# A two-layer transformer block: more convolution taps on TensorE, over shifted copies of the input, and a gate chunk moved ahead

## The reference, cut to what matters

```python
def odd_mixer(h, w_in, dw_w, dw_b, ln_g, ln_b, w_out):
    proj = h @ w_in                                     # [512, 3 * 1024]
    a, b, gate = jnp.split(proj, [CONV_WIDTH, 2 * CONV_WIDTH], axis=-1)
    glu = a * jax.nn.sigmoid(b)
    conv = lax.conv_general_dilated(                    # depthwise, causal, 31 taps
        glu, dw_w.astype(glu.dtype), window_strides=(1,), padding=[(CONV_K - 1, 0)],
        dimension_numbers=('NWC', 'WIO', 'NWC'), feature_group_count=CONV_WIDTH)
    cf = conv.astype(jnp.float32) + dw_b.astype(jnp.float32)
    ...                                                 # layer norm of cf over the 1024 channels
    y = jax.nn.silu(cn).astype(h.dtype) * jax.nn.silu(gate)
    return y @ w_out
```

## Time and profile before

| | us |
|---|---|
| median of 3 runs (lowest to highest) | 1125.66 (1124.29 to 1127.17) |
| the profiled execution, its own time | 1125.93 |
| its span in the profile | 1124.1 |
| PE busy | 1033.6 (92%) |
| DVE busy | 584.4 (52%) |
| ACT busy | 468.5 (42%) |
| POOL busy | 170.0 (15%) |

### The profile page before, as it was taken

One profiled execution on the slowest core, in us unless ns is written; L12 is line 12 of the kernel. 1 busy time (PEld: TensorE's weight loads), 2 busy tenths in 40 slices (PEclk: granted clock), 3 DMA queues, 4 the chain that ended last, 5 costly groups with the idle time before them and its releaser, 6 DMA issues.

```text
span 1124.1 us, 12285 instructions
## 1 busy us (share of the span) xinstructions
PE 1033.6 (92%) x4847; PEld 824.7 (73%) x4847; DVE 584.4 (52%) x768; ACT 468.5 (42%) x765; POOL 170.0 (15%) x131
## 2 busy tenths in 40 slices
PE   3899999997999999999999979989898899979897
PEld 2677677886788888888888868767677667657676
DVE  5436665235744234333344463366556397777853
ACT  3325562135533334134123354234355557556541
POOL 2200101000000000000000000022000189886300
PEclk8999999998999999999999999989999799999989
DMA  6532102034221252233224214302033222210301
GB/s 213 73 122 76 38 1 76 1 113 150 76 76 75 75 187 75 75 109 116 76 75 149 76 38 132 141 1 75 2 136 120 68 76 76 75 54 27 145 1 75
DMA packets 55823, 93.91 MB, mean 84 GB/s; under 512 B 2581, under 2 KB 23958, under 8 KB 55638
## 3 DMA queue, kind: packets, MB, share of 16 engines
q1 hardware_dynamic: 53648, 90.61, 23.3%
q10 hardware_dynamic: 2118, 2.52, 1.6%
HBM read 90.76 MB, written 2.36 MB: 83 GB/s over the span
## 4 chain that ended last, share of the span: by engine, by line
PE 55%; DVE 8%; ACT 4%; issue 3%; POOL 1%; DMA 1%; SPq 0%; DVEq 0%; POOLq 0%; ACTq 0%
PE acc L702 17%; PE acc L703 17%; PE acc L704 16%; DVE wlr L1768 2%; ACT wh L1362 2%; DVE psT L2113 1%; POOL pacc L1295 1%; PE psT L861 1%; DMA wl<-in_c_w_in_dram 1%; PE ps L861 1%; PE ps L993 1%; DVE rt L1795 1%; DVE act_lo L1812 1%; ACT junk L1391 1%; PE psT L978 1%
## 5 line engine op out<-in xcount | busy, mean ns | idle before, releaser
L1768 DVE TENSOR_TENSOR wlr<-wl,wh 128x2048 fp32r<-128x2048 f32 (+1 forms) x66 | 149.9, 2276 | 96.4 <-ACT wh L1362 96.4
L702 PE MATMUL acc<-act_hi,wh 128*128 128x512 f32 x464 | 187.9, 405 | 1.7 <-DVE act_lo L1812 1.4
L704 PE MATMUL acc<-act_hi,wlr 128*128 128x512 f32 x464 | 182.3, 393 | 0.0
L703 PE MATMUL acc<-act_lo,wh 128*128 128x512 f32 x464 | 182.1, 392 | 0.0
L1362 ACT ACTIVATE wh<-wl 128x2048 fp32r<-128x2048 f32 (+1 forms) x66 | 123.7, 1880 | 61.2 <-DMA wl<-in_w_up_dram 35.1
L702 PE MATMUL acc<-wh,act_hi 128*128 128x512 f32 x320 | 131.3, 410 | 19.0 <-DVE act_lo L1738 7.6
L703 PE MATMUL acc<-wlr,act_hi 128*128 128x512 f32 x320 | 127.6, 399 | 0.0
L704 PE MATMUL acc<-wh,act_lo 128*128 128x512 f32 x320 | 127.6, 399 | 0.0
L1295 POOL TENSOR_TENSOR pacc<-pacc,prod 128x512 f32<-128x512 f32 x80 | 117.5, 1469 | 28.6 <-ACT prod L1644 16.1
L702 PEld LDWEIGHTS acc<-act_hi,wh 128*128 128x128 f32 x464 | 88.4, 191 | 21.7 <-DVE act_lo L1812 1.8
L703 PEld LDWEIGHTS acc<-act_lo,wh 128*128 128x128 f32 x464 | 88.3, 190 | 19.1 <-issue 1.7
(11 more groups left out here) (221 smaller groups left out, 1536.8 us busy)
## 6 DMA issues: line engine op xcount, KB each, us to landing
wl<-in_w_up_dram SPq DMA_DIRECT2D x16, 1024.0 KB, 6.3
wl<-in_w_down_dram SPq DMA_DIRECT2D x16, 1024.0 KB, 6.3
raw<-in_w_in_dram SPq DMA_DIRECT2D x18, 512.0 KB, 4.8
wl<-in_a_w_in_dram SPq DMA_DIRECT2D x8, 1024.0 KB, 6.2
wl<-in_c_w_in_dram SPq DMA_DIRECT2D x16, 512.0 KB, 6.2
wl<-in_w_out_dram SPq DMA_DIRECT2D x4, 1024.0 KB, 6.2
wl<-in_ab_w_out_dram SPq DMA_DIRECT2D x4, 1024.0 KB, 7.4
wl<-in_c_w_in_dram SPq DMA_DIRECT2D x4, 1024.0 KB, 6.4
```

The lines of the kernel that those rows point to most:

```text
L702: pe.matmul(dst, hi, x_hi, start=first, stop=False)
L703: pe.matmul(dst, hi, x_lo, start=False, stop=False)
L704: return pe.matmul(dst, lo, x_hi, start=False, stop=last)
L1768: dve.tensor_tensor(wlr[slot][:, kk, cols], wl[slot][:, kk, cols], wh[slot][:, kk, cols].bitcast(F32), ALU.subtract).then_inc(wlo_done, 1)
```

## The change

Five edits, all quoted from the diff.

**1. Taps.** TensorE takes 16 taps instead of 4, DVE 15 instead of 16, ACT and GpSimd none. The 16 taps are four passes of four taps. A pass works on 32 channels at a time: the 128 rows of the array are 4 taps by 32 channels, the 128 x 32 weight `tapw` has on each of its four 32 x 32 blocks the diagonal of one tap, and the result goes to 32 partitions of PSUM. The moving operand needs four copies of the 32 channels' `glu`, each shifted by one token more, on different partitions: that is the new tile `shifted`, written from `glu` by 16 DMAs for each channel tile, issued by SP.

```diff
-PE_TAPS = 4
-DVE_TAPS = 16
-ACT_TAPS = TAPS - DVE_TAPS - PE_TAPS
+PE_TAPS = 16
+PASSES = PE_TAPS // 4
+Y_TAPS = 8
+X_TAPS = TAPS - PE_TAPS - Y_TAPS
+SHIFTED = 4 * (PASSES - 1) + TOK
...
             def conv_taps(t):
 
-                pe.wait_ge(evD_done, evacs_before(TILE_AT[N_AB, 0], "D") + t + 1)
-                pe.wait_ge(diag_done, PE_TAPS * (t + 1))
-                if t >= 2:
-                    pe.wait_ge(conv_done, t - 1)
-                for m in range(PE_TAPS):
-                    j = TAPS - PE_TAPS + m
-                    last = pe.matmul(vacc(t, 0), diag[:, t % 2, m, :], glu[:, t % 4, j:j + TOK],
-                                     start=m == 0, stop=m == PE_TAPS - 1)
+                pe.wait_ge(shift_in[t % 2], 16 * 16 * (t // 2 + 1))
+                pe.wait_ge(tapw_done, t + 1)
+                if t >= 3:
+                    pe.wait_ge(conv_done, t - 2)
+                for m in range(PASSES):
+                    for c in range(4):
+                        last = pe.matmul(xsum(t)[32 * c:32 * c + 32, :], tapw[:, t % 2, 4 * m + c, :],
+                                         shifted[:, t % 2, c, 4 * m:4 * m + TOK], start=m == 0, stop=m == PASSES - 1)
                 last.then_inc(petap_done, 1)
...
+            def shift(t):
+
+                sp.wait_ge(evD_done, evacs_before(TILE_AT[N_AB, 0], "D") + t + 1)
+                if t >= 2:
+                    sp.wait_ge(petap_done, t - 1)
+                for c in range(4):
+                    for j in range(4):
+                        sp.dma_start(shifted[32 * j:32 * j + 32, t % 2, c, :],
+                                     glu[32 * c:32 * c + 32, t % 4, j:j + SHIFTED]).then_inc(shift_in[t % 2], 16)
```

**3. The shift in SP's order.** The copies of a tile stand in SP's program among the loads of weights:

```diff
+            load_chunk(N_AB + 1, c_in, ((0, 256, CW), (CW, D + 256, CW)))
+            shift(0)
+            load_chunk(N_AB + 2, c_in, ((0, 512, CW), (CW, D + 512, CW)))
+            shift(1)
+            shift(2)
+            load_chunk(N_AB + 3, c_in, ((0, 768, CW), (CW, D + 768, CW)))
+            shift(3)
+            shift(4)
             load_chunk(N_G1, c_in, ((0, 2 * D + 512, 512),))
+            shift(5)
+            shift(6)
             load_chunk(N_CO0, a["c_w_out_2"][0], ((0, 0, 512),))
+            shift(7)
```

```diff
-N_AO0, N_AO1, N_AB, N_G0, N_G1, N_CO0, N_CO1 = 23, 24, 25, 29, 30, 31, 32
+N_AO0, N_AO1, N_G0, N_AB, N_G1, N_CO0, N_CO1 = 23, 24, 25, 26, 30, 31, 32
...
+            for b in range(NBLK):
+                block_turned(2, b)
+                token_tile(N_G0, b, 0)
+                if b < 2:
+                    turn_block(2, b + 2)
+                token_tile(N_G0, b, 1)
...
+            after = {0: 5, 1: 6, 3: 7}
+            for b in range(NBLK):
+                token_tile(N_G1, b, 0)
+                if b == 1:
+                    conv_taps(KT - 1)
+                token_tile(N_G1, b, 1)
+                if b in after:
+                    turn_conv(after[b])
```

```diff
+            def lo_following(n):
+
+                for piece in range(2):
+                    kk, cols = slice(4 * piece, 4 * piece + 4), slice(0, chunk_width(n))
+                    pool.wait_ge(whi_done, piece_count(n, piece))
+                    pool.wait_ge(wlo_done, piece_count(n, piece) - 1)
+                    pool.tensor_tensor(wlr[n % 2][:, kk, cols], wl[n % 2][:, kk, cols],
+                                       wh[n % 2][:, kk, cols].bitcast(F32), ALU.subtract).then_inc(wlo_done, 1)
...
-                    if b in (1, 2):
-                        hi(following, b - 1)
+                    if b in ((1, 2) if s == 2 else (0, 1)):
+                        hi(following, b - (s == 2))
...
-                    if b >= 2:
-                        lo(following, b - 2)
```

More of the change, by code:

```diff
@@ L85, in all_tiles @@
         tiles += [(n, b, b, "D") for b in range(NBLK)]
-    for n in range(N_AB, N_G0):
+    tiles += [(N_G0, b, b, "A") for b in range(NBLK)]
+    for n in range(N_AB, N_AB + 4):
         tiles += [(n, m, m, "AD"[m % 2]) for m in range(4)]
-    for n in (N_G0, N_G1, N_CO0, N_CO1):
+    for n in (N_G1, N_CO0, N_CO1):
         tiles += [(n, b, b, "A" if n < N_CO0 else "D") for b in range(NBLK)]
@@ L109, in chunk_dmas @@
 def chunk_dmas(n):
-    return 2 if N_AB <= n < N_G0 else 1
+    return 2 if N_AB <= n < N_AB + 4 else 1
 def chunk_width(n):
@@ L167, in shape_constants @@
     return np.concatenate([np.eye(P), np.ones((P, P)), fwd, bwd, restart,
-                           np.broadcast_to(cnt, (P, 64))], axis=1).astype(np.float32)
+                           np.broadcast_to(cnt, (P, 64)), np.tile(np.eye(32), (4, 1))], axis=1).astype(np.float32)
 def alibi_band():
@@ L235, in block_kernel @@
         act_lo = sb("act_lo", [P, KT, TOK], F32R)
+        R_off = top[0]
         R = sb("R", [P, TOK])
@@ L1182, in _ @@
                         turn_conv(after[i, m])
-            after = {(0, 1): 5, (1, 0): 6, (1, 2): 7}
-            for i in range(2):
-                for b in range(NBLK):
-                    token_tile(N_G0 + i, b, 0)
-                    if i == 0 and b == 0:
-                        conv_taps(KT - 1)
-                    token_tile(N_G0 + i, b, 1)
-                    if (i, b) in after:
-                        turn_conv(after[i, b])
+            after = {0: 5, 1: 6, 3: 7}
[6 more added lines that the diff above has]
+                    turn_conv(after[b])
             for b in range(NBLK):
@@ L1278, in _ @@
                 mixer_step_pool(1, step)
+            lo_following(N_G0)
             pool.wait_ge(ob_done, 4)
@@ L1656, in _ @@
                 half_square(2, 0, b)
-            boundary_blocks(2, N_AB)
+            boundary_blocks(2, N_G0)
             act.wait_ge(taps_ps, 1)
-            act.activation(taps[:, :, :], ps6[:, 0:KT * TAPS].rearrange("p (k t) -> p k t", k=KT), ACT.Copy)\
-               .then_inc(taps_done, 1)
-            act.wait_ge(taps_done, 1)
+            act.activation(taps_all[:, :], ps6[:, 0:KT * TAPS + P], ACT.Copy).then_inc(taps_done, 1)
+            for b in range(NBLK):
+                gate_out(N_G0, b)
+            hi(N_AB, 0)
+            hi(N_AB, 1)
             sigmoid(0)
@@ L2090, in gated @@
                 if t >= 4:
[L2091 to L2092 removed]
+                    dve.wait_ge(shift_in[t % 2], 16 * 16 * (t // 2 - 1))
+                    dve.wait_ge(x_step, X_TAPS * (t - 3))
                 dve.tensor_tensor(glu[:, t % 4, CPAD:], acc[:, TILES[e][2], :], sg[:, t % 2, :], ALU.mult)\
                    .then_inc(evD_done, 1)
[L2096 to L2115 removed]
@@ new lines, in y_tap @@
+            def y_tap(t, i):
+                src, sums = glu[:, t % 4, PE_TAPS + i:PE_TAPS + i + TOK], ysum[:, t % 2, :]
+                scale = taps[:, t, PE_TAPS + i:PE_TAPS + i + 1]
+                if i == 0:
+                    dve.wait_ge(evD_done, evacs_before(TILE_AT[N_AB, 0], "D") + t + 1)
+                    if t >= 2:
+                        dve.wait_ge(conv_done, t - 1)
+                    ins = dve.tensor_scalar(sums, src, scale, vec[:, V_DWB + t:V_DWB + t + 1], ALU.mult, ALU.add)
+                else:
+                    dve.wait_ge(y_step, Y_TAPS * t + i)
+                    ins = dve.scalar_tensor_tensor(out=sums, in0=src, scalar=scale, in1=sums, op0=ALU.mult, op1=ALU.add)
+                ins.then_inc(y_step, 1)
@@ L2117, in conv_sum, with x_tap @@
+            def x_tap(t, i):
+                j = PE_TAPS + Y_TAPS + i
+                if i == 0:
+                    dve.wait_ge(petap_done, t + 1)
+                else:
+                    dve.wait_ge(x_step, X_TAPS * t + i)
+                dve.scalar_tensor_tensor(out=xsum(t), in0=glu[:, t % 4, j:j + TOK], scalar=taps[:, t, j:j + 1],
+                                         in1=xsum(t), op0=ALU.mult, op1=ALU.add).then_inc(x_step, 1)
             def conv_sum(t):
-                dve.wait_ge(padd_done, ACT_TAPS * (t + 1))
```

216 lines of the change are left out of this document (89 added, 127 removed).

## The result

| | before | after |
|---|---|---|
| median of the runs, us | 1125.6 (1124.3 to 1127.2, 4 runs) | 1214.9 (1209.0 to 1216.5, 4 runs) |
| profiled execution, its span | 1124.1 | 1211.7 |

The changed kernel takes 1.078 times as long (95% interval 1.075 to 1.081). The forecast of 1178 had the sign right and the time 37 us short, within the range of 1146 to 1232. The spans differ by 87.6 us, where the sum said 52.

What follows compares the result with a forecast made beforehand. TensorE, busy 92%, was taken as the bound, its waits paid in full. Shift waits 60 + clock 17 - old waits 16 - passages 4, 5.5 and 5.5 + layer norm 6 = +52 on 1125.9: 1178 us, range 1146 to 1232.

Steps and rivals of the forecast that it cites:

- The shift: At the taps, TensorE waits for glu, 16 SP issues and landing, less half a tile: 60 us added over eight tiles.
- The clock: After seven waits of about 8 us at the taps TensorE runs at 1.2 GHz, losing 2.4 us each: +17 us.
- The old waits and their clock: First a/b to last gate tile: 11.2 us of waits at the taps and about 5 of low clock go, 16 us won.
- Passages: Waits for low halves and normalised blocks, with their low clock, shrink at three passages: 4, 5.5 and 5.5 us won.
- I take it as hidden: First two passages: GpSimd's 4.5 us low half costs nothing, its input coming a block earlier; if late, at most 7 us back.
- Rival D: GpSimd's low halves late, DVE still asked for them: at most 9.5 us back; 4%, 1130 to 1148 with other middle ways.
- The third passage's bare chain of 4.9 us: Ahead of the first a/b tile TensorE idles for tile read-out 0.7, high half 1.9 and low half 2.3 us.
- The layer norm: After the last gate tile the chain from last transpose to first normalised block lies bare, 10.4 us against 4.3 idle: +6 us.
- Taps: TensorE's 16 column-quarter taps run four at once, judged by the state products (L1044): 3.6 us per tile, no change in work.
- Rival A: Shifted copies arrive within the half tile, so no wait or clock loss is left: 1101 us, chance 6%.
- rival C's larger end: Waits at the taps larger: 0.55 us per issue, copies queueing behind weights at three tiles, upper clock bound: about 1205; 77% with smaller and middle.

Runs made afterwards that it cites:

- the best version: Changed kernel with copies on two queues ahead of weights, taps a tile later, low halves on DVE, two waits moved: 1098.9 us, 0.976 of the kernel before.
- the run with two queues: Changed kernel with ACT's queue issuing half of each tile's 16 copies, SP the other half, weights still ahead: 1190.1 us, ratio 1.058 to the kernel before.

## Why the prediction was right, and where it was wrong

**The shift: right in mechanism and order, 60 us for 77.5 measured.** The chain `glu`, sixteen issues, landing, less the half tile, is what the trace shows. The term that was mis-sized is the pitch: "Nothing suggests that a smaller DMA is issued faster" was true, but "The last of 16 starts 15 x 0.48 = 7.2 us after the first" became 9.5 (0.63 us each), slower than both rows that I had averaged. That is 2.3 us at each of eight tiles, 18 us. The landing was 2.0 instead of 2.6, 5 us the other way. With both, even tiles should wait 0.7 + 9.5 + 2.0 - 2.7 = 9.5 us, and they waited 9.0 to 9.6. The Trainium skill's formula (DMA: Bandwidth & Descriptors, Anatomy of one DMA), 2.15 us, was nearer to the landing than my row of the output, though it is given for DMAs of GpSimd and these are SP's. At t = 1 and 3 I had 1.3 us for the weights ahead, and they cost 3.0 and 2.7. At t = 1 the copies began 2.0 us later, since the four weight issues took 2.67 us, and their own issues slowed (11.0 us for sixteen). At t = 3 they began 1.4 us later, and the last took 3.0 us to land. At t = 7 it was 5.4 for 2.5.

**The clock: +17 for 19.0 measured.** "2.4 each" is right: 38.0 us at half rate over eight waits. It was seven waits in the sum and eight in the trace. The old waits and their clock, 16 us, went as stated: 77.5 - 11.2 + 19.0 - 5 = 80.3, the stretch's difference. That this closes to the digit is chance, since the low clock at the stretch's own start (2.7 us lost before, 1.6 now) is left out of it.

**Passages: -15 predicted, +2.8 measured, the step that failed.** It was "I take it as hidden". I looked at whether GpSimd would be ready when TensorE asks, and it was. I did not ask what its 4.6 us do to DVE beside it, whose normalisation I had myself named as what "comes last next". The price given there for its failure, 7 us back if GpSimd were late, was for another mechanism, and the miss was more than twice that: 7 us of it come back when the halves return to DVE, the rest is gain that never came. By place, -9.5 was forecast for the first two passages: from 258.6 to the first block turned of the third (857.3) the changed kernel takes 2.7 us more than before (259.8, 855.8). For the third -5.5 was forecast, and from that block to the first a/b tile, without the 21.7, it takes 1.3 us more. It was there to be had, with the halves in another order and the high halves of the first a/b chunk moved ahead: in the best version the first a/b tile starts at 881.4 with the 21.7 us of `N_G0` ahead of it, 18 us better than before (877.8 + 21.7 = 899.5). Rival D (low halves late) is out; its neighbour, DVE held up by them, came true. The third passage's bare chain of 4.9 us ahead of the first a/b tile came out to the digit:

```profile
902.30 0.79 PE L721 MATMUL acc<-act_hi,wh 128*128 128x512 f32 x1 [4.91 <-DVE wlr L1776]
```

but the other side of that sum did not: 3.5 us of waiting for `un` stayed there, and GpSimd held up DVE's `un` and `rt` there too (861.11, 864.28).

**The layer norm: +6 predicted, +4.5 measured.** The end of the chain in the changed kernel, against the earlier trace rows:

```profile
1143.46 0.60 PE L869 MATMUL ps<-ident_ones,ct 128*128 128x128 f32 x4
1152.64 1.97 PE L859 MATMUL psT<-ident_ones,un 128*128 128x128 f32 x8 [8.58 <-DVE un L2192]
```

9.2 us from the last transpose to the first block turned, where I carried over 10.4 from before; the chain is bare, as said.

**Taps: 3.6 us per tile, as predicted** from the row of L1044. The 2.38-fold of three column tiles in the Trainium skill (TensorE: Matmul & The Clock Gate, part 3) would have made it 4.5 us; 16 matmuls of 0.9 in 3.57 us are a factor of 4.0.

**The sum.** Waits +17.5, clock +2, passages +18, layer norm -1.5 make the 36 us between 52 and 87.6. Rival A fell: every tile but the last kept TensorE waiting 9 us or more. Of rival C's larger end, 0.55 us per issue was too low, and copies queueing behind the weights were seen in the run with two queues. That the range held is in part luck: two errors of about 18 us both fitted under its upper end, which had been set for other things.

## What to carry to other kernels

A data shuffle by DMA costs its count of issues times the pitch of the queue, plus one landing; set that sum against the work that stands between producer and consumer before writing it, and close a gap in three ways: another issuing queue, nothing ahead of it in the queue, the consumer later. If the other queue is that of an engine with work of its own, count the issues there too: eight of them kept ACT from its next instruction for 5.3 us. When work moves to GpSimd, ask not only whether it is done in time but which VectorE instructions with two SBUF operands run beside it, for each of them may be held up for the whole instruction. And before giving work to another engine, try the same work one step earlier on its own: here that won 11 us with two edited conditions.
